# A hybrid Mamba-2 / mixture-of-experts layer on one core: six rows of the conditioning vector are summed piece by piece on VectorE during the mixer

## The reference, cut to what matters

```python
cs = jax.nn.silu(c)                                # (1, D)
mod = cs @ w_ada[i] + b_ada[i]                     # (1, 6 * D)
sh1, sc1, g1, sh2, sc2, g2 = jnp.split(mod, 6, axis=-1)
hm = x * (1.0 + sc1) + sh1
y = mamba2_mixer(hm, ...)                          # 8 groups, chunked scan, gated norm, @ w_out
x = layer_norm(ALPHA * x + (1.0 + g1) * y, ln_g[0], ln_b[0])
hm = x * (1.0 + sc2) + sh2
y = grouped_moe(hm, ...)                           # 32 experts, top 2
x = layer_norm(ALPHA * x + (1.0 + g2) * y, ln_g[1], ln_b[1])
```

## Time and profile before

| | |
|---|---|
| median of three runs | 3170.24 us (3162.49 to 3171.62) |
| the profiled execution's own time | 3165.22 us |
| its span, first to last instruction | 3163.5 us |
| TensorE busy | 2831.0 us, 89% |
| VectorE busy | 2187.7 us, 69% |
| ScalarE busy | 1290.2 us, 41% |
| GpSimd busy | 1521.8 us, 48% |

### The profile page before, as it was taken

How to read it: one execution, slowest core, us unless ns; L and a number is a source line. 1 busy time by engine, 2 the same in 40 slices (tenths; PEclk the granted TensorE clock), 3 DMA queues, 4 the chain that set the end, 5 groups by cost and what they waited for, 6 DMA issues and landing times. The chain is left out here.

```text
span 3163.5 us, 41657 instructions
## 1 busy us (share of the span) xinstructions
PE 2831.0 (89%) x14910; PEld 2351.3 (74%) x14910; DVE 2187.7 (69%) x2565; ACT 1290.2 (41%) x1591; POOL 1521.8 (48%) x819
## 2 busy tenths in 40 slices
PE   7599999999999999999767999967999999999920
PEld 2289888888888888889625888855888888888810
DVE  2468777687777877777522333356888888888868
ACT  1233333333433333333221111104776776777722
POOL 0023334433343333343300222214899999999965
PEclk9799999999999999999878999987999999999965
DMA  6753535434454445443082332217987879677667
GB/s 234 298 203 134 188 149 189 155 120 174 170 187 156 154 156 181 154 164 123 30 330 80 113 106 106 106 57 274 341 311 279 298 253 337 227 285 276 245 237 243
DMA packets 253157, 618.50 MB, mean 196 GB/s; under 512 B 14946, under 2 KB 97506, under 8 KB 244324
## 3 DMA queue, kind: packets, MB, share of 16 engines
q1 hardware_dynamic: 226820, 521.35, 45.6%
q10 hardware_dynamic: 14688, 53.48, 4.2%
q0 software_dynamic: 11520, 41.95, 3.9%
HBM read 609.13 MB, written 99.88 MB: 224 GB/s over the span
## 5 line engine op out<-in xcount | busy, mean ns | idle before, releaser
L1494 DVE TENSOR_TENSOR piece_lo<-piece_raw,piece_hi 128x2048 fp32r<-128x2048 f32 x187 | 564.0, 3035 | 102.6 <-ACT piece_hi L1599 102.5
L1599 ACT CAST piece_hi<-piece_raw 128x2048 fp32r<-128x2048 f32 x280 | 526.8, 1913 | 203.5 <-DVE ye L1659 157.2
L1494 POOL TENSOR_TENSOR piece_lo<-piece_raw,piece_hi 128x2048 fp32r<-128x2048 f32 x93 | 567.7, 6105 | 25.1 <-ACT piece_hi L1599 21.9
L565 PE MATMUL pj<-hm,w_hi 128*128 128x512 f32 x2048 | 531.7, 405 | 24.2 <-DMA hm<-hm_parts 22.1
L824 DVE SCALAR_TENSOR_TENSOR cv<-ub,par,cv 128x512 f32<-128x512 f32 x384 | 385.4, 1004 | 208.8 <-ACT cv L712 199.8
L565 PEld LDWEIGHTS pj<-hm,w_hi 128*128 128x128 f32 x2048 | 378.3, 190 | 99.4 <-DMA hm<-hm_parts 23.7
L529 POOL TENSOR_TENSOR xw<-xw,t 128x512 f32<-128x512 f32 x64 | 96.9, 1514 | 475.1 <-DVE t L900 475.1
L580 PE MATMUL pz<-wz_hi,hm 128*128 128x256 f32 x2048 | 294.8, 289 | 0.4
L580 PEld LDWEIGHTS pz<-wz_hi,hm 128*128 128x128 f32 x2048 | 264.6, 191 | 6.2 <-DVE wz_lo L802 3.2
L717 ACT ACTIVATE th<-cv 128x512 f32<-128x512 f32 x128 | 81.2, 634 | 436.3 <-DVE cv L824 436.3
L565 PE MATMUL pj<-hm,w_lo 128*128 128x512 f32 x1024 | 254.8, 391 | 0.0
(11 more groups left out here) (287 smaller groups left out, 5970.2 us busy)
## 6 DMA issues: line engine op xcount, KB each, us to landing
hm<-hm_parts SPq DMA_DIRECT2D x32, 4096.0 KB, 13.3
piece_raw<-in_w_gate SPq DMA_DIRECT2D x94, 1024.0 KB
piece_raw<-in_w_up SPq DMA_DIRECT2D x94, 1024.0 KB
piece_raw<-in_w_down SPq DMA_DIRECT2D x92, 1024.0 KB
decay<-acum_rows SPq DMA_DIRECT2D x32, 1024.0 KB, 4.7
w_raw<-in_w_in SPq DMA_DIRECT2D x48, 512.0 KB, 7.5
expert_out<-ye ACTq DMA_DIRECT2D x46, 512.0 KB, 6.6
hm_parts<-hl SPq DMA_DIRECT2D x4, 4096.0 KB, 16.1
```

The source lines that it names most:

```text
L565: mm = nc.tensor.matmul(pj[m % 2][:], wp[m][:, kk, :], hm[b][:, hp, kk, :], start=q == 0, stop=q == 3 * KK - 1)
L1494: v.tensor_tensor(lo[q][:], raw[q][:], hi[q][:].bitcast(F32), ALU.subtract).then_inc(lo_done[q], 1)
L1599: nc.scalar.copy(hi[q][:], raw[q][:]).then_inc(hi_done[q], 1)
```

## The change

- Host side: `w_ada` keeps its first 2048 columns; the other 4096 are handed over transposed, as `w_ada_t` (4096 x 1024), and c also as a row.
- Mixer: after its six first weight pieces, SyncE loads c into every partition (`cs_row`); ScalarE makes its tanh, VectorE two operations that turn it into silu(c). In every super-step SyncE loads 128 rows of `w_ada_t` (512 KB) and VectorE multiplies them by `cs_row` and sums along the row, in one `tensor_tensor_reduce` whose sums go to a column of `k.ada` (128 x 32: piece n is column n).
- To make room in memory, the tanh results `th` and `zth` and the squares `sq` have no tiles of their own any more: tanh goes straight into the tile that VectorE then overwrites, squares into `t1`. Waits that guard these tiles move from VectorE to ScalarE.
- Row stage: no `w_ada`. ScalarE turns four columns of `k.ada` into four diagonal 128x128 tiles (`diag`), one product by a tile of ones sums each column of it into all partitions, VectorE adds the bias row as before. `w_out` has six buffers and is issued by SyncE, ahead of the bias rows; VectorE's order is new.
- One small index table is dropped (`eidx`; `tidx` holds the same numbers).

The core of the diff:

```diff
@@ mixer_steps, SyncE
+            def ada_load(n):
+                sp.wait_ge(ada_done, n)
+                sp.dma_start(wada[:], k.d["w_ada_t"][n * P:(n + 1) * P, :]).then_inc(ada_in, 16)
...
             for n in range(RAW, PIECES):
                 piece(n)
+            sp.dma_start(csr[:], k.d["c_row"][0].partition_broadcast(P)).then_inc(c_in, 16)
+            sp.wait_ge(csr_done, 2)
+            sp.dma_start(wada[:], k.d["w_ada_t"][0:P, :]).then_inc(ada_in, 16)
             sp.wait_ge(zero_set, 1)
...
                 if i >= 1:
                     store(i - 1, 0)
+                if 1 <= i < STEPS:
+                    ada_load(i)
@@ mixer_steps, ScalarE
             def tanh(i, m):
+                j = i - 1
+                if m == 0 and j >= 0:
+                    act.wait_ge(b_tr, j + 1)
+                    act.wait_ge(g_mm, j + 1)
...
                 act.wait_ge(tap, 3 * (CONV * i + m + 1))
-                nc.scalar.activation(th[m % 2][:], cv[m % 2][:], ACT.Tanh).then_inc(th_done, 1)
+                nc.scalar.activation((bx, cx[i % 2], x0, x1)[m][:], cv[m % 2][:], ACT.Tanh).then_inc(th_done, 1)
...
             for n in range(PIECES):
                 high(n)
+            act.wait_ge(c_in, 16)
+            nc.scalar.activation(wada[:], csr[:], ACT.Tanh, scale=0.5).then_inc(c_th, 1)
@@ mixer_steps, VectorE
+            def ada(n):
+                dve.wait_ge(ada_in, 16 * (n + 1))
+                nc.vector.tensor_tensor_reduce(out=wada[:], in0=wada[:], in1=csr[:], scale=1.0, scalar=0.0,
+                                               op0=ALU.mult, op1=ALU.add, accum_out=k.ada[:, n:n + 1]
+                                               ).then_inc(ada_done, 1)
             for n in range(PIECES):
                 low(n)
+            dve.wait_ge(c_th, 1)
+            nc.vector.scalar_tensor_tensor(out=wada[:], in0=wada[:], scalar=1.0, in1=csr[:], op0=ALU.add, op1=ALU.mult
+                                           ).then_inc(csr_done, 1)
+            dve.wait_ge(csr_done, 1)
+            nc.vector.tensor_scalar(csr[:], wada[:], 0.5, None, ALU.mult).then_inc(csr_done, 1)
+            dve.wait_ge(csr_done, 2)
             for i in range(STEPS + 1):
                 j, here = i - 1, i < STEPS
                 if j >= 0:
                     gates(j, 1)
+                    ada(j)
@@ row_vectors
-        NW = 3
+        NW = 6
...
+            def spread(s):
+                if s >= 2:
+                    act.wait_ge(row_mm, s - 1)
+                for q in range(4):
+                    nc.scalar.activation(diag[s % 2][:, q * P:(q + 1) * P], k.ident[:], ACT.Copy,
+                                         scale=k.ada[:, 4 * s + q:4 * s + q + 1]).then_inc(diag_done, 1)
+            spread(0)
+            spread(1)
             for m in range(YTILES):
                 act.wait_ge(wo_in[m % NW], 16 * (m // NW + 1))
                 nc.scalar.activation(w_hi[:, m, :], ...)
+                if m + 2 < NR:
+                    spread(m + 2)
...
             for s in range(NR):
-                pe.wait_ge(wr_in[s % 2], 16 * (s // 2 + 1))
+                pe.wait_ge(diag_done, 4 * (s + 1))
                 if s >= 2:
                     pe.wait_ge(row_out, s - 1)
-                for kk in range(KK):
-                    mm = nc.tensor.matmul(rp[s % 2][:], csb[:, kk, :], wa[s % 2][:, kk, :],
-                                          start=kk == 0, stop=kk == KK - 1)
-                mm.then_inc(row_mm, 1)
+                nc.tensor.matmul(rp[s % 2][:], k.ones[:], diag[s % 2][:], start=True, stop=True).then_inc(row_mm, 1)
...
+            low(0)
+            low(1)
+            dve.wait_ge(bias_in, 16 * (NR + 2))
+            for s in range(NR):
+                row(s)
+                low(2 + s)
```

More of the change, by code:

```diff
@@ L389, in mixer_steps @@
         bs = sb("bs", [P, SUBS, P])
-        zth = sb("zth", [P, 2, GW])
         zs = [sb(f"zs{b}", [P, SUBS, GW]) for b in range(2)]
@@ L985, in row_vectors @@
         block = ctx.enter_context(nc.Block())
-        w_ada = k.d["w_ada"].rearrange("(kk p) n -> p kk n", p=P)
         @block.sync
         def _(sp):
+            for m in range(NW):
+                sp.dma_start(wraw[m][:], k.d["w_out"][m * P:(m + 1) * P, :]).then_inc(wo_in[m], 16)
             for n, row in enumerate(rows):
@@ L1042, in low, with row @@
                                                ).then_inc(lo_done, 1)
-            dve.wait_ge(bias_in, 16 * (len(rows) + 2))
-            for s in range(NR):
-                for m in range(s * YTILES // NR, (s + 1) * YTILES // NR):
-                    low(m)
+            def row(s):
                 dve.wait_ge(row_mm, s + 1)
```

98 lines of the change are left out of this document (40 added, 58 removed).

## The result

The changed kernel took 3117.74 us (median of 4 runs, 3111.78 to 3122.31), the kernel before on the same chip 3167.45 (4 runs, 3162.49 to 3171.62): the ratio is 0.9852, its 95% interval 0.9838 to 0.9865. The forecast was 3118.5, with a range of 3105 to 3134. The profiled execution of the changed kernel took 3118.38 us, its span is 3116.6 us, 46.9 us less than before.

What follows compares the result with a forecast made beforehand. TensorE was taken to bound the mixer, `w_ada` loads and waits the row stage. Row stage -52.9 and mixer's start +1.2 gave -51.7 us: 3113.5 profiled, 3118.5 us as median, range 3105 to 3134.

Steps and rivals of the forecast that it cites:

- The sum costs nothing: Each super-step: VectorE's 1.5 us multiply-and-sum fits its 6.40 us gap and ends three to five us before the taps.
- Load and moved waits cost nothing: Super-steps: the 512 KB load avoids the decay rows' load, and moved waits are met in time; cost nothing.
- The mixer's start, +1.2 us: Mixer's start: ScalarE's extra tanh of 1.15 us delays TensorE's waiting unit; 2.5 if the row of c takes 6.9 us.
- The row stage, -52.9 us: Row stage without `w_ada`: VectorE ends at 1629.5 us, where it was 1682.4.
- B: Row stage: the time the wait for all bias rows ends, 1599.0 us, after 6.29 MB at 391 GB/s.
- VectorE's work behind B: Row stage from B on: 8 pieces, 14 tiles and five products, together 27.9 us.
- The stall: Row stage behind B: VectorE idles 2.0 us before its third tile and 0.6 over the next three, 2.6 us.
- the next three tiles cost ScalarE 2.15 us each against VectorE's 1.93: 0.6 more: Row stage, tiles behind VectorE's third: ScalarE's longer time for each adds 0.6 us of VectorE idle time.
- The rest is the first 20 us and gaps between the loads.: Old row stage of 103.3 us: 28.3 MB take 72 us, the rest being the first 20 us and load gaps.
- The sum of the forecast: Whole kernel: -52.9 + 1.2 = -51.7 us, 3113.5 against the profiled 3165.2; 3118.5 for a median, which lies 5.0 higher.
- The rivals: Row stage gives less, 3125 to 3128, 0.10; sum doesn't fit, 3137, 0.06; slower, 3190, 0.04; nothing net, 3168, 0.02.
- The slower rival: Super-steps: the sum takes 6.7 us and ends 2.3 us late 31 times, 71 us, 3190; chance 0.04.

Runs made afterwards that it cites:

- no_sums: Changed kernel without the 31 later loads of transposed weights and all 32 multiply-and-sums; super-steps 1359.1 us against 1355.8, profiled execution 3155.25 us (other experts).
- plus3: Changed kernel with three more VectorE operations of 128x1024 ahead of each multiply-and-sum; 3126.38 us.
- before_one_product: Kernel before, with one of the eight products of each `w_ada` piece and all loads; row stage 85.6 us against 105.1, profiled execution 3182.32 us (other experts).
- best2: Changed kernel with c loaded behind the first hm, bias rows issued earlier and eight diagonal tiles; 3105.22 us, ratio 0.9817 to the kernel before.
- eight_diag2: Changed kernel with eight diagonal tiles in place of two; row stage 47.6 us against 53.7, profiled execution 3113.24 us.
- plus6: Changed kernel with six more VectorE operations of 128x1024 ahead of each multiply-and-sum; 3264.62 us.
- rows_first2: Changed kernel, SyncE issuing two `w_out` tiles, eight bias rows, four tiles, then norm rows; row stage 47.6 us against 53.7, profiled execution 3110.31 us.

## Why the prediction was right, point by point

- **The sum costs nothing.** Right, and shown from both sides: without it the super-steps are no shorter (no_sums), and three more operations of its size cost at most 0.2 us a super-step (plus3). Its price was taken as 1.5 us, measured 1.22 and 0.08 for the read-out, overlapping. The load took 3.9 us in the median and 5.3 at the longest, where 4.5 to 6.9 were allowed for.
- **Load and moved waits cost nothing.** Right: 1.3 us of waits for the load in all, TensorE at 174.90 of 175 us, and the super-steps as long as before.
- **The mixer's start, +1.2 us.** The step itself held (c at 162.26 for a forecast of 161.7, the third unit 1.3 us later against the first product). It priced a wait by its length alone; that TensorE may pay at 1.2 GHz for the products behind it was left out. Between the two executions compared the term is 3.85 us, 2.6 of them the clock; but before is the fastest of the three executions with its start. By the means of three and seven executions the term is 1.9 us, so it was mis-sized by 0.7.
- **The row stage, -52.9 us.** Measured -51.4; by VectorE's last row, where the forecast ends, 52.3 us for a forecast of 50.4, thus -51.0. B came out to the tenth (19.9 us into the stage), which is in part luck: the forecast was 3.8 us without flow and then 391 GB/s, measured are 311 GB/s over the first 12.5 us and 407 over the next 7.5. Here the Trainium skill, "DMA: Bandwidth & Descriptors", section "Where 436 GB/s comes from", by its figure of about 358 GB/s per core, had B 1.5 us later in the prediction's estimate. That estimate kept the start of the flow at 1582.9, which was itself reckoned with 391; with 358 in both places B comes, as an estimate, only 0.4 us later, so B can't tell the two rates apart. The stretches do: besides the 407, before_one_product and best2 flow at 394 and 395 GB/s in 40 and 18 us. VectorE's work behind B was 26.6 us for a forecast of 27.9. The stall was mis-sized: 5.8 us in place of 2.6. The step that failed is "the next three tiles cost ScalarE 2.15 us each against VectorE's 1.93: 0.6 more". It compared the two engines' loads and overlooked that they are tied in a ring by two buffers; these tiles cost 3.0, where best2, without the ring, has 0.33 for each. The diagonals were 1.28 us for four, not 1.0, and a product up to 2.05, not 1.7: the rest of it, 2.8 for 2.0 at the first tile. eight_diag2 shows that nothing but ScalarE's work behind B made VectorE wait.
- **"The rest is the first 20 us and gaps between the loads."** This reading of the old stage, bytes with gaps, told only half. In the first 20 us the bytes already flow (391 GB/s from 1582.5 on the earlier trace rows). What comes on top of the 72 us are 4 us at the start, three gaps of 4 us and the last 18 us, from 1666 on, when nothing is left to load and TensorE and VectorE finish. Products and bytes each held the stage up nearly as long: leaving out six of the eight loads gave 19 us. The forecast came right because the change takes away both, and because the new stage was priced from its own parts.
- **The sum of the forecast.** In the profiled executions the change is -46.8 us for a forecast of -51.7: 2.6 from the start, 1.5 from the row stage, and 0.7 net of the other stages, all within their spread. The 5.0 us that were added to get from the profiled execution to a median made up for it: after's profiled execution lies at its median. By the medians of the result the gain is 49.7 us, 2.0 less than forecast, and before's own median came out at 3167.45, 2.8 under the 3170.24 that the forecast started from. The two errors cancel, so 3118.5 against 3117.74 is closer than the steps deserve.
- **The rivals.** None came: the row stage gave 1.5 us less and not 6, and the sum ends 5.3 us before the taps in the super-step shown. The slower rival's price law, about a microsecond on the path for one of delay, held in plus6; its condition, a delay of 1.7 us a super-step, was far off.

## What to carry to other kernels

Work that is moved into a gap of an engine costs nothing as long as it ends before the operation that the bound engine waits for; measure how much room is left by adding more of the same, and see what else runs there: beside GpSimd's products the same operation took 1.94 us in place of 1.22. Where bytes and products alternate, taking one away may give only a part (19 us of 51 here), since it bares the other. Engines that are tied in a ring through two buffers can cost more than the busiest of them (here 3.0 us over three tiles, 1.0 by load alone). And where TensorE waits 2 to 4 us, carry the chance that the products behind it run at the lower clock; one pair of executions can't size that, several with the same code can.

## What the runs showed of the hardware that was not expected

- A multiply-and-sum of 128x1024 takes as long as a plain product (1221 and 1222 to 1225 ns), and reading the sum out 84 ns.
- The same VectorE operation takes 1.22 us alone and 1.94 beside GpSimd's products, which grow from 1.04 to 2.02 us.
- After a wait of 2 to 4 us TensorE's granted clock fell in some executions and not in others: 16 products took 6.50 us behind a wait of 3.26, 3.91 behind one of 3.40, and 5.41 behind one of 2.17 (in ten executions with the start of before or after the clock held in two).
- With eight products of 1.97 us in such a wait the clock stayed at 1.00 in the one execution in which they were tried; so it did without them in rows_first2.
